# Forward and backward scan of an RWKV-7 mixer run in common hops, with undecayed states and another order of the pieces

## What is computed

```python
def step(S, inp):
    w_t, k_t, v_t, a_t, b_t = inp[:5]
    sa = einsum('dbhij,dbhj->dbhi', S, a_t)
    S = S * w_t[..., None, :] + sa[..., :, None] * b_t[..., None, :] + v_t[..., :, None] * k_t[..., None, :]
    return S, einsum('dbhij,dbhj->dbhi', S, inp[5])        # read with r_t
# decay = exp(-exp(w_log)); a = -kk; b = kk * a_rate; output: y[0] + flip(y[1]),
# then a group norm over each head, + (r . k_dir * r_k) v, * gate, @ w_out
```

## Time and profile before

| what | value |
|---|---|
| median of 3 runs | 2483.46 us (2478.06 to 2487.39) |
| the profiled execution: its own time | 2489.29 us |
| its span, first to last instruction | 2487.2 us |
| busy over the span | PE 92%, DVE 44%, ACT 35%, POOL 26% |
| granted TensorE clock, mean | 0.983 of 2.4 GHz |
| first `pre` product (L1225) of slot 0 and of slot 15 | 1275.6 us, 1952.2 us |
| last product of the last scan (L1624) | 2073.8 us |

### The profile page before, as it was taken

How to read it: one execution, slowest core, us unless ns; L and a number is a source line. 1 busy time by engine, 2 the same in 40 slices (tenths; PEclk the granted TensorE clock), 3 DMA queues, 4 the chain that set the end, 5 groups by cost and what they waited for, 6 DMA issues and landing times.

```text
span 2487.2 us, 65185 instructions
## 1 busy us (share of the span) xinstructions
PE 2297.5 (92%) x27583; PEld 1901.2 (76%) x27583; DVE 1104.8 (44%) x2425; ACT 866.5 (35%) x1579; POOL 657.5 (26%) x481
## 2 busy tenths in 40 slices
PE   5998899899999999999988888888988889999998
PEld 3776677788888888878847777776776767888887
DVE  4236666351121112463366666666666645411213
ACT  3435555342121213352234334344244222422323
POOL 0334555212232332213311211111111110344442
PEclk8999999999999999999999999999999999999999
DMA  8125555112211221123410000000000011323321
GB/s 250 52 56 162 174 170 170 52 51 68 66 59 62 67 68 51 52 82 113 140 47 23 21 8 21 12 15 23 12 15 23 4 53 52 100 87 101 101 89 64
DMA packets 172316, 176.37 MB, mean 71 GB/s; under 512 B 26512, under 2 KB 160032, under 8 KB 172064
## 3 DMA queue, kind: packets, MB, share of 16 engines
q1 hardware_dynamic: 171200, 169.48, 21.8%
q10 hardware_dynamic: 864, 3.15, 0.3%
HBM read 161.06 MB, written 11.53 MB: 69 GB/s over the span
## 4 chain that ended last, share of the span: by engine, by line
PE 83%; DVE 7%; issue 5%; ACT 2%; SPq 1%; DMA 1%; POOL 1%; ACTq 0%; DVEq 0%
PE PS L397 38%; PE PS L1480 5%; PE PS L558 5%; PE PS L417 3%; PE PS L1465 2%; PE PS L756 2%; PE PS L737 2%; PE PS L1619 2%; PE PS L1455 2%; PE PS L1292 2%; PE PS L716 2%; PE PS L1564 1%; PE PS L746 1%; PE PS L1594 1%; PE PS L1123 1%
## 5 line engine op out<-in xcount | busy, mean ns | idle before, releaser
L377 POOL TENSOR_TENSOR WL<-RAW,WH 128x1024 fp32r<-128x1024 f32 x160 | 383.6, 2419 | 945.3 <-ACT WH L358 945.3
L397 PE MATMUL PS<-AH,WH 128*128 128x256 f32 (+1 forms) x992 | 350.8, 354 | 3.3 <-DVE AL L2358 2.4
L397 PE MATMUL PS<-AH,WL 128*128 128x256 f32 (+1 forms) x992 | 351.7, 355 | 0.0
L397 PE MATMUL PS<-AL,WH 128*128 128x256 f32 (+1 forms) x992 | 349.1, 352 | 0.0
L358 ACT ACTIVATE WH<-RAW 128x1024 fp32r<-128x1024 f32 x160 | 159.9, 1047 | 272.4 <-PE PS L397 265.7
L397 PE MATMUL PS<-BH,WL 128*128 128x512 f32 (+1 forms) x672 | 239.2, 356 | 0.0
L397 PE MATMUL PS<-BH,WH 128*128 128x512 f32 (+1 forms) x672 | 238.5, 355 | 0.0
L397 PE MATMUL PS<-BL,WH 128*128 128x512 f32 (+1 forms) x672 | 237.6, 354 | 0.0
L397 PEld LDWEIGHTS PS<-AH,WH 128*128 128x128 f32 x992 | 187.7, 189 | 31.6 <-issue 2.6
L397 PEld LDWEIGHTS PS<-AL,WH 128*128 128x128 f32 x992 | 187.0, 188 | 27.1
L397 PEld LDWEIGHTS PS<-AH,WL 128*128 128x128 f32 x992 | 187.4, 189 | 25.3
(11 more groups left out here) (270 smaller groups left out, 4874.6 us busy)
## 6 DMA issues: line engine op xcount, KB each, us to landing
ADW<-l_ada_w SPq DMA_DIRECT2D x40, 1024.0 KB, 5.3
RAW<-l_mlp_up SPq DMA_DIRECT2D x64, 512.0 KB, 4.5
RAW<-l_mlp_down SPq DMA_DIRECT2D x64, 512.0 KB, 4.0
RAW<-l_w_rkv SPq DMA_DIRECT2D x24, 512.0 KB, 5.2
rwkv_scratch<-STG SPq DMA_DIRECT2D x24, 384.0 KB, 3.4
ADA<-l_ada_w SPq DMA_DIRECT2D x4, 2048.0 KB, 12.1
RAW<-l_w_in SPq DMA_DIRECT2D x16, 256.0 KB, 5.4
RAW<-l_w_out SPq DMA_DIRECT2D x16, 256.0 KB, 5.3
```

The source lines that it names most:

```text
L377: e.tensor_tensor(WL[:, s, rows], RAW[:, s, rows], WH[:, s, rows], ALU.subtract).then_inc(w_split[h], 1)
L397: mm = e.matmul(dst, w[:, s, k, n * P:(n + 1) * P], r[:, k, lo:hi], start=(k == 0 and i == 0), stop=(k == KT - 1 and i == 2), skip_group_c ...
```

## The change

- **Common hops.** The forward scan of a group and the backward scan of the group before or of the same group run side by side. Slot s now has `hops(s)` hops: 4 in even slots, 8 in odd ones, and each does both directions (`runs`). There are 100 hops in place of 192, with the same products: each PE piece holds the products of two scans. A unit's scan is now spread over two slots (forward 4 + 8, backward 8 + 4), so there are 19 slots, and the last four hops are of the backward scan alone.
- **On DVE** a hop has one add for both directions (RH, 128 columns), the copy of the forward correction, and one operation for each direction on the state. The copy of the backward correction is on ACT (`delta_copy`).
- **Undecayed states.** SS is kept without the last chunk's decay; the factor is applied when the next state is formed, `SS' = SS * total + new`. SW and L1715 go. In exchange AR is multiplied by the totals once for each unit, on POOL, behind its masks (`DECAYED`), and a small copy TOT holds the totals.
- **Buffers.** AR, BKT and MT come in fours, WP in twos. XIF and LV are gone: the inverse goes into the first 64 columns of MT, LV into the second 64 (three ACT copies in place of one). `chain_freed` guards the reuse.
- **Elsewhere.** The transposes of the values move behind those of the keys. The product with HEAD1 of the r*k row (it was in the tail) moves into `pre` of the odd unit, with the DVE product behind it; its result waits in X and OG. The gate weights have one buffer and a load of their own.
- **Order.** The two strings SLOT are replaced: 89 and 97 letters (33 p, 40 i, and 16 or 24 c) in place of 114 and 114 (33 p, 40 i, 41 c).

```diff
-        SLOT = (("ipciciiciippcipcpcipicicicpiciciccicpccicicpipcicpicpicpicip"
+        SLOT = (("ipcipcipicpipicipcipipcipicipcipipcipicpicipipcipipipciipipi"
...
-            for s in range(NQ + 2):
+            for s in range(NQ + 3):
-                         "c": iter(chain(e, s - 2)) if s >= 2 else iter(())}
+                         "c": iter(chain(e, s)) if s >= 2 else iter(())}
...
+        def hops(s):
+            return 0 if s < 2 else 8 if s % 2 else 4
+        def runs(s, i):
+            both = ((0, s - 3, 4 + i), (1, s - 2, i)) if s % 2 else ((0, s - 2, i), (1, s - 3, 8 + i))
+            return [(d, q, j, ORDER[d][j]) for d, q, j in both if 0 <= q < NQ]
+        def delta_copy(e, op, s, i, d):
+            for r, q, j, c in runs(s, i):
+                if r == d:
+                    o = HALVES[1 - c % 2]
+                    e.wait_ge(sa_done, hop(s, i) + 1)
+                    op(VSA[q // 2 % 2][o, c, :].rearrange("p (h v) -> p h v", h=2),
+                       pair(5).rearrange("p (h v) -> p h v", h=2)[o, :, 3 * HD:4 * HD]).then_inc(sa_ready[d], 1)
...  pool_pre
+            e.wait_ge(mat_done, 6 * q + 6)
+            e.wait_ge(ar_step, 2 * q + 1)
+            for lo, hi, wide, t0 in DECAYED[d]:
+                ins = e.tensor_tensor(AR[b][:, lo:hi, 0:wide, :]..., AR[b][...], totals(q)[...].to_broadcast(...), ALU.mult)
+            ins.then_inc(ar_step, 1)
...  act_pre
-            e.activation(LV[b][:, :, :, :]..., pair(3)..., ACT.Copy).then_inc(lv_ready, 1)
+            for u, m0, m1 in ((0, 0, 2), (4, 2, 4), (8, 4, 6)):
+                ins = e.activation(lv(b, u), sums[:, m0:m1], ACT.Copy)
+            ins.then_inc(lv_ready, 1)
...  dve_chain
-                    e.tensor_tensor(RH[:, :], bank(5)[:, 0:HD], LV[b][:, cp, m, :], ALU.add).then_inc(rh_ready, 1)
-                        e.tensor_scalar(SW[:, :], SS[:, j % 2, :], total, None, ALU.mult).then_inc(sw_ready, 1)
+                        e.tensor_tensor(RH[:, :, :], pair(5)...[:, :, 0:HD], MT_ALL[:, first:first + 2 * step]...[:, :, 0:HD], ALU.add)
+                            ins = e.scalar_tensor_tensor(out=SS[:, 1 - i % 2, d, :], in0=SS[:, i % 2, d, :],
+                                                         scalar=totals(q)[:, before:before + 1], in1=new, op0=ALU.mult, op1=ALU.add)
...  act_chain
-            if q == NQ - 1:
+                if s == NQ + 1 and i == 4:
...                 (the weights' high part, L1668 before, and out_high of three blocks, L1650 before)
+                delta_copy(e, lambda o, x: e.activation(o, x, ACT.Copy), s, i, 1)
```

More of the change, by code:

```diff
@@ L218, in two @@
             return [core(f"{name}{i}", shape, dt) for i in range(2)]
-        def three(name, shape, dt=F32):
-            return [core(f"{name}{i}", shape, dt) for i in range(3)]
         KK = core("KK", [P, T])
@@ L1333, in act_pre @@
             yield
-            if d == 0:
-                e.wait_ge(vt_done, g + 1)
-                for cp, t in enumerate(HALVES):
-                    ins = e.activation(VSA[gp][t, cp::2, :], pair(3)[t, 0:T].rearrange("p (m c) -> p m c", c=P), ACT.Copy)
-                ins.then_inc(vt_ready, 1)
             yield
@@ L1612, in pe_chain @@
                 if last:
[L1613 removed]
+                    direct_early(e, 3 * (n - hop(NQ + 1, 0)) + 1, 1)
                 yield
[L1615 removed]
+                for d in range(2):
+                    finished(e, s, i, d)
                 e.nop(nofuse=True)
[L1617 to L1621 removed]
@@ new lines, in pe_chain @@
+                if mm is not None:
+                    mm.then_inc(st_done, 1)
+                for d, q, j, c in now:
+                    if j >= NCH - NX:
+                        for h, k in enumerate(HEADS):
+                            mm = e.matmul(bank(7)[k, c * C - TC:(c + 1) * C - TC], VSA[q // 2 % 2][:, c, k],
+                                          mt(q % 4, 2 * (c // 2) + h, 2 + c % 2), start=False, stop=(d == 1),
+                                          skip_group_check=True)
+                        if j == NCH - 1:
+                            mm.then_inc((forward_done, y_done)[d], 1)
@@ new lines, in dve_chain, with par @@
+        def dve_chain(e, s):
+            for i in range(hops(s)):
+                n = hop(s, i)
+                now = runs(s, i)
+                going = [(d, q, c) for d, q, j, c in now if j]
+                if going:
+                    e.wait_ge(rhs_done, n)
+                    at = sorted((MT_PLACE[q % 4] * MT_W + mt_at(c) + C, rh_at(s, d)) for d, q, c in going)
+                    (first, x), (second, y) = at[0], at[-1]
+                    if len(going) == 2:
+                        assert (x, y) == (0, 1)
+                        step = second - first
+                        e.tensor_tensor(RH[:, :, :], pair(5).rearrange("p (x v) -> p x v", x=2)[:, :, 0:HD],
+                                        MT_ALL[:, first:first + 2 * step].rearrange("p (x v) -> p x v", x=2)[:, :, 0:HD],
+                                        ALU.add).then_inc(rh_ready, 1)
+                    else:
+                        e.tensor_tensor(RH[:, x, :], bank(5 + x)[:, 0:HD], MT_ALL[:, first:first + HD],
+                                        ALU.add).then_inc(rh_ready, 1)
+                yield
+                delta_copy(e, e.tensor_copy, s, i, 0)
+                yield
+                ins = None
+                for d, q, j, c in now:
+                    if j < NCH - 1:
+                        e.wait_ge(st_done, n + 1)
+                        new = bank(6)[:, (4 + d) * HD:(5 + d) * HD]
+                        if j:
+                            e.wait_ge(st_ready, n)
+                            before = ORDER[d][j - 1]
+                            ins = e.scalar_tensor_tensor(out=SS[:, 1 - i % 2, d, :], in0=SS[:, i % 2, d, :],
+                                                         scalar=totals(q)[:, before:before + 1], in1=new, op0=ALU.mult,
+                                                         op1=ALU.add)
+                        else:
+                            ins = e.tensor_copy(SS[:, 1, d, :], new)
+                if ins is not None:
+                    ins.then_inc(st_ready, 1)
+                yield
+            if s % 2 == 0 and s >= 4:
+                g = (s - 4) // 2
+                half = TX // 2
+                def par(name):
+                    return col(1, ROWS_B[name] + g)
```

370 lines of the change are left out of this document (198 added, 172 removed).

## The result

The changed kernel takes 2499.63 us (median of 5 runs, 2497.39 to 2506.12) against 2481.08 of the kernel before in the runs beside them: ratio 1.008 [1.0057, 1.0103]. It is slower by 18.6 us; 2433 (2400 to 2475) was predicted. The profiled execution has a span of 2497.7 us, 10.5 more than before: the execution traced before the change (2489.29) lay 8.2 above the 2481.08 of these runs, so the traces show some 10 of the 18.6 us.

The account below looks back on a forecast made before the run. PE was taken as the bound, with holes. Gains of 41.6 us (steady slots), 7.1 (slot 2) and 10.5 (slot 16), less 8.8 at the end, gave 50.4; 2489.3 less that and 5.8 made 2433 us, range 2400 to 2475.

Parts of the forecast that it names:

- Rival 1: Steady slots: the even order removes over half of PE's waits, 3.2 us more a slot, 2391 us; chance 0.13.
- rival 3: Double hops, slots 3 to 15: backward copy waits in ACT's queue, 0.9 us a hop, 2506 us; chance 0.10.
- Fewer pieces on PE: Steady slots: 17.25 fewer chain pieces at 0.10 us a turn save 1.7 us a slot (0 to 3.1).
- Fewer waits in the chain: Steady slots: with half the hops, half of the chain's 1.6 us of waits goes, 0.8 a slot (0 to 1.6).
- DVE relief: Steady slots: 5.9 us less DVE work gains 1.2 us a slot where DVE is the limit (0 to 1.7).
- The boundary: Between slots: the next pre product waits for LV's copy, 0.5 us lost a slot (0 to 1).
- POOL: New multiplications on POOL: some 3.0 us a unit, covered before XIT is needed, price 0 (up to 3.0 a slot).
- Slot 2: Slot 2: four hops of one scan in place of twelve, 8 x 0.89 = 7.1 us gained.
- slot 16: Last inverse with four hops for twelve: 34.0 us in place of 44.5, 10.5 gained (4 to 14).
- The last twelve hops: Slots 17 and 18: two-scan pieces and the copy behind ACT's block (3.9 us) lose 8.8 us (4 to 14).
- a sign of being wrong: Steady slots: the forecast is wrong if the steady slot stays above 46.5 us; 44.3 was forecast.

Follow-up runs that it names:

- e3: Changed kernel with the four tail pieces c12 to c15 moved to the last third of the even string; 2482.45 us, 0.9973 of the kernel before.
- e10: Changed kernel with the even string's second half rewritten: masked products behind the tail's Ln and Exp, c15 behind the last mask; 2475.01 us, 0.9968 of the kernel before.
- e4: Changed kernel with four inverse pieces in place of one between p6 and the key-rate piece p7 in the even string; 2517.0 us, 1.0123 of the kernel before.
- e5: Changed kernel with both correction copies on DVE and two fitted strings, chain pieces behind the key rates, tail late; 2493.14 us, 1.0049 of the kernel before.
- e2: Changed kernel with the backward correction's copy on DVE instead of ACT; 2499.6 us, 1.0066 of the kernel before.
- e7: Changed kernel with POOL's multiplication of AR done twice for each unit; 2498.85 us, 1.0069 of the kernel before.
- e12: Changed kernel with the values transposed ahead of the keys, as before, in slot 0 only; 2495.94 us, 1.0057 of the kernel before.
- e15: e10 with the values of group 0 transposed early in slot 0, no useless products; 2467.21 us, 0.9933 of the kernel before.
- e8: Changed kernel without steady-slot table loads, Ln and Exp replaced by Exp and copies, values wrong; 2489.24 us, 1.003 of the kernel before.

## Why the prediction was wrong

- **The order: the step that failed.** The sum let PE's idleness in a steady slot fall by 1.5 us (0.8 in the chain and 1.2 on DVE, less 0.5 at the boundary) and had no term for what the new strings do to it. It rose by 2.7 us, from 5.9 to 8.7. Rival 1 took evenness for a help and said of the tail's Ln, Exp and table loads that they "keep their place beside the inverse"; they do not, they moved from the end of the odd slots into the even ones. In rival 3, "three others" between two chain pieces counted as cover, but all three are p and i pieces, and i waits for ACT itself. In the kernel before, a hop of PE and DVE alone lay under ACT's key rates; that could be seen in ACT's timeline laid beside PE's, and in the old strings, where chain pieces crowd around p7. Shown for the tail by e3 and e10: a new second half for one string is worth 25 us, more than the whole loss. For the key rates the wait is shown (2.5 us in each even slot), but neither e4 nor e5 turned it into time.
- **Fewer pieces on PE**: right in kind, too small. -1.7 us a slot predicted; PE's busy time fell by 2.05, and in e10, at the clock of the kernel before, by 3.2. That the turns are what went is argued, not shown. (The 0.015 us a product in the upper end of this term stands in no row, and a steady slot has 18 pieces; 18.75 holds the two ends of the scan as well.)
- **Fewer waits in the chain**: wrong. 0.8 us a slot were to go; the waits before L1685 alone are 1.6 a slot (12.1 and 4.2 us for L1803 and L1807), where the three of the earlier trace rows made 1.6. The waits before the update went (none in the ten slots, one of 0.8 us in the last hops), and others of the same sum stand at the hop's second trip.
- **DVE relief**: 5.9 us of its busy time a slot were to go, 3.8 went (306.9 to 269.0 in ten slots). That any of it came back as time no run shows: e2 gives DVE 17.5 us of it back (286.5 for 269.0) and is not slower. (The RH part of the 5.9, 1.3 us, stands in no row.)
- **The boundary**: right. 0.5 predicted, 0.6 measured (L1242, 6.2 us in eleven places).
- **POOL**: right for the changed kernel. The multiplication is 1.90 us for 1024 columns (2.5 was the bound from the earlier trace rows), and e7 gives it no price; under the order of e10 it holds DVE up. (The double hops of slots 3 to 15 are 80, not 81, which makes rival 3's loss 72 us in place of 73.)
- **Slot 2** gave 3.9 of 7.1, slot 16 6.4 of 10.5 (38.1 us for the 34.0 predicted). The last twelve hops cost 6.4 of 8.8: ACT's block ahead of hop 4 is there as foreseen, but PE waited 0.8 us behind it and not 3.9, since the early products ran under it.

```profile
2057.75 2.00 ACT L1765 ACTIVATE WH<-RAW_THIRD 128x1024 fp32r<-128x1024 f32 x2
...
2061.19 0.40 ACT L1738 ACTIVATE AH<-OG 128x256 fp32r<-128x256 f32 x1
2061.61 0.27 ACT L1768 ACTIVATE VSA<-PS 64x128 f32<-64x128 f32 x1
```

- **Not foreseen**: slots 0 and 1, 10.2 us together. The values' transposes account for some 7 of them in the trace of e12, for 4 in its time.

The steady slots were to give 3.2 us each. The sum now reads: 2.05 from PE's work, less 2.7 of new idleness. The steady slot takes 48.2 us, above the 46.5 that the prediction named as a sign of being wrong. In e10 the sum reads 3.2 from PE's work, less 1.8 of idleness (59.4 us before, 77.1 in the ten slots): even with the tail in a better place the idleness did not fall, and the kernel gains 8 to 16 us (e10, e15) of the 50. Of the changed kernel's idleness the three waits of an even slot are 2.50 + 1.69 + 3.27 = 7.5 us, 3.7 for each slot of a pair, and smaller waits went in return.

The waits taken away never gave their whole length (in the ten slots e3 gave 15.6 of 25 us, e8 7.5 of 15.5). Part comes back as other waits: the idleness fell by 9.5 us in e3 and by 10.5 in e8. The rest is PE's busy time, which fell by 6.1 in e3, where the clock rose, and grew by 3.0 in e8, where it did not. What stays open: why the idleness stays above that of the kernel before in every order tried, and which order would give the whole 50 us, if any does.

## What to carry to other kernels

When an order written by hand looks uneven, find what each crowd of pieces covers before spreading it: list the long blocks of every engine (table loads, tails) and see which pieces run beside them and need none of that engine. If a change takes pieces away, or moves a block into another slot, holes can open, and the gain of the change and the price of the new order must be costed together. Here a change that saved work on the bound engine paid only once the order was fitted to it. And when waits are counted, look at the busy time of the same instructions too: a part of what a wait costs can stand there.
